# Sample attention with half, sample and head on the partitions, and sample values by column tiles of the PE array

## The reference, cut to what matters

```python
# sample group: DEC_SEQ = 1, 128 samples, 4 heads of 128, 256 memory tokens
qh = q.reshape(bn, t, XA_HEADS, XA_HEAD_DIM)
s = jnp.einsum('bthd,bmhd->bhtm', qh, mem_k)
p = jax.nn.softmax(s * (1.0 / math.sqrt(XA_HEAD_DIM)), axis=-1)
o = jnp.einsum('bhtm,bmhd->bthd', p, mem_v).reshape(bn, t, XA_WIDTH)
z_c = (o * jax.nn.silu(qg)) @ xa_wo
y = (g_a * z_a + g_b * z_b + g_c * z_c) @ w_out
```

## Time and profile before

| | us |
|---|---|
| runs before (median of 3) | 780.32 (775.95 to 801.77) |
| profiled execution, its own time | 778.57 |
| span of its slowest core (core 4) | 777.0 |
| spans of the eight cores | 770.2 to 777.0 |
| granted TensorE clock, core 4 | 0.985 of full |
| busy: PE / PE weight loads / DVE / ACT / POOL | 727.6 / 459.4 / 398.3 / 344.8 / 246.0 |

### The profile page before, as it was taken

One profiled execution on the slowest core, in us unless ns is written; L12 is line 12 of the kernel. 1 busy time (PEld: TensorE's weight loads), 2 busy tenths in 40 slices (PEclk: granted clock), 3 DMA queues, 4 the chain that ended last, 5 costly groups with the idle time before them and its releaser, 6 DMA issues.

```text
span 777.0 us, 13244 instructions; the slowest of 8 cores (770.2 to 777.0 us)
## 1 busy us (share of the span) xinstructions
PE 727.6 (94%) x4884; PEld 459.4 (59%) x4884; DVE 398.3 (51%) x379; ACT 344.8 (44%) x408; POOL 246.0 (32%) x303
## 2 busy tenths in 40 slices
PE   2887999989999989989999999999999999999995
PEld 1555656556566546646666656666666666665442
DVE  3444253747849529727975865546321221223675
ACT  4346378687694776777661211121211112112332
POOL 5555101202103002102023344435464554523211
PEclk9999999999999989989999999999999999999998
DMA  9998934422613322412333694655895848226833
GB/s 201 187 191 148 135 72 40 41 24 19 54 17 35 34 26 28 41 11 29 38 38 72 96 182 80 101 112 65 112 111 68 109 55 74 26 109 217 288 149 139
DMA packets 112618, 69.47 MB, mean 89 GB/s; under 512 B 93987, under 2 KB 100213, under 8 KB 112539
## 3 DMA queue, kind: packets, MB, share of 16 engines
q0 software_dynamic: 99808, 31.60, 40.3%
q1 hardware_dynamic: 12747, 37.03, 14.4%
HBM read 90.53 MB, written 9.82 MB: 129 GB/s over the span
## 4 chain that ended last, share of the span: by engine, by line
PE 84%; DMA 6%; ACT 3%; DVE 2%; issue 2%; POOL 1%; POOLq 0%; SPq 0%; ACTq 0%; DVEq 0%
PE PP L644 72%; PE PP L1211 8%; DMA R<-xp 3%; DMA R<-w_in 3%; PE PP L989 2%; ACT R L847 1%; PE PP L981 1%; DVE R L834 1%; PE PP L1075 1%; ACT R L984 1%; PE PP L1114 0%; POOL R L692 0%; POOL R L702 0%; ACT R L698 0%; PE PP L770 0%
## 5 line engine op out<-in xcount | busy, mean ns | idle before, releaser
L644 PE MATMUL PP<-R 128*128 128x344 bf16 x4104 | 619.7, 311 | 7.7 <-ACT R L847 4.0
L644 PEld LDWEIGHTS PP<-R 128*128 128x128 bf16 x4104 | 399.4, 98 | 216.1 <-issue 19.4
L1163 ACT ACTIVATE R<-PP 128x688 f32<-128x688 f32 x72 | 53.5, 743 | 221.1 <-PE PP L644 188.3
L134 POOL DMA_DIRECT2D R<-w_in x68 | 61.5, 905 | 276.6 <-PE PP L644 265.3
L1172 DVE SCALAR_TENSOR_TENSOR R<-R,PP 128x688 f32<-128x688 f32 x72 | 62.6, 871 | 151.1 <-PE PP L644 137.0
L1211 PE MATMUL PP<-R 128*128 128x512 bf16 (+1 forms) x272 | 59.0, 379 | 0.0
L1176 POOL TENSOR_TENSOR R<-R 128x688 f32<-128x688 f32 x24 | 39.4, 1641 | 36.8 <-DVE R L1172 35.9
L1211 PEld LDWEIGHTS PP<-R 128*128 128x128 bf16 (+1 forms) x272 | 26.4, 97 | 32.3 <-issue 0.4
L834 DVE SCALAR_TENSOR_TENSOR R<-R 128x2048 f32<-128x2048 f32 x18 | 42.3, 2349 | 5.4 <-ACT R L831 4.4
L1181 POOL TENSOR_TENSOR R<-R 128x688 bf16<-128x688 f32 x24 | 39.0, 1641 | 18.4 <-DVE R L1172 18.0
L1220 ACT ACTIVATE R<-R 128x1024 f32<-128x1024 f32 (+1 forms) x17 | 18.0, 1057 | 46.3 <-DVE R L1215 46.3
(11 more groups left out here) (131 smaller groups left out, 592.5 us busy)
## 6 DMA issues: line engine op xcount, KB each, us to landing
R<-w_in POOLq DMA_DIRECT2D x68, 256.0 KB, 5.9
R<-xp SPq DMA_DIRECT2D x32, 512.0 KB, 6.1
R<-ck SPq DMA_DIRECT2D x16, 512.0 KB, 4.4
y_p<-R SPq DMA_DIRECT2D x16, 512.0 KB, 2.9
R<-cv POOLq DMA_DIRECT2D x16, 256.0 KB, 7.4
R<-w_out POOLq DMA_DIRECT2D x8, 256.0 KB, 7.9
R<-xa_wo POOLq DMA_DIRECT2D x14, 128.0 KB, 4.9
R<-lru_wo POOLq DMA_DIRECT2D x8, 192.0 KB, 4.0
```

Of the source, the lines that this page charges most:

```text
L134: eng.dma_start(out=out, in_=in_).then_inc(sems[semkey], 16)
L644: return lambda e: e.matmul(ps.ap[:, b * 512:b * 512 + BLK], lhs(k), rhs[:, k, c:c + BLK], start=(k == 0), stop=(k == nk - 1))
L1163: G.act(lambda e, ps=pg[u], th_=th_: e.activation(out=b3(th_.ap), in_=pv(ps), func=AF.Tanh, scale=0.5), UW, [pg[u].tok], [th_.tok], Px - E ...
```

## The change

Scores: keys come from the host in another layout, so that one load holds 16 tokens of every sample, with token half, sample and head on the 128 partitions (2 x 16 x 4) and 8 tokens x 128 dimensions in each row of 4 KB. The queries are put in that order by two copies and one transpose after the fourth head (`tq`, `qs`, 128 x 128). The multiply reads `qs` from SBUF and repeats it over 8 tokens; the spreading matmuls and the first pair of transposes are gone. The second half's scores are moved from partitions 64 to 127 to 0 to 63 by one DMA within SBUF (`sall`).

Values: each load is again one sample, in rows of 4 KB. `Pm` is widened to 32 columns for each sample, zero but for the 4 columns of its heads. For each four samples 32-column weights from `Pm` stand in four column groups (partitions 32g to 32g + 31 of the PSUM tile), and the values are the moving side, 512 columns: 8 matmuls for four samples, 32 in all. Four results are added up in `Os`, transposed by four 32-bit transposes and gated by four small VectorE operations. There are 7 value buffers in place of 8. Some small tiles move: `qs` now shares space with `pretmp` (L780) and `Ps`, `Pm` with `Sall` and `Es`.

```diff
@@ -432,8 +432,8 @@
     xp = din("xp", [T, D])
     xs = din("xs", [TS, D])
     memp = din("memp", [NM, D])
-    ck = din("ck", [TS, NM, XW])
-    cv = din("cv", [TS, NM, XW])
+    ck = din("ck", [TS, 128, 1024])
+    cv = din("cv", [TS, 128, 1024])
     st_h = din("st_h", [TS, W])
     st_lc = din("st_lc", [TS, 3 * W])
     st_sc = din("st_sc", [TS, 2 * W])
@@ -552,20 +552,21 @@
         m_cinp = front("cinp", 2 + TT, F32)
         SIDE = cur["p"]
         NJS = 6
-        PERM = RB - (XW * 2 + 512 + 256 + 2048 + NJS * TS * 8)
+        PERM = RB - (3072 + NJS * TS * 8)
         assert SIDE + 24672 <= PERM, (SIDE, PERM)
 
         def side(name, off, n, dt):
             return Mem(name, SIDE + off, n, dt)
 
         m_a2 = side("a2", 0, TT, F32)
-        m_qs = Mem("qs", PERM, XW, BF16)
-        m_Sall = Mem("Sall", PERM + 1024, 128, F32)
-        m_Pm = Mem("Pm", PERM + 1536, 128, BF16)
-        m_Es = Mem("Es", PERM + 1792, 256, F32)
-        m_Ps = Mem("Ps", PERM + 2816, 256, F32)
-        m_thS = Mem("thS", PERM + 3840, NJS * TS, F32)
-        m_acS = Mem("acS", PERM + 3840 + NJS * TS * 4, NJS * TS, F32)
+        m_tq = Mem("tq", PERM + 1024, 128, BF16)
+        m_qs = Mem("qs", PERM + 2048, 128, BF16)
+        m_Sall = Mem("Sall", PERM, 256, F32)
+        m_Es = Mem("Es", PERM + 1024, 256, F32)
+        m_Ps = Mem("Ps", PERM + 2048, 256, F32)
+        m_Pm = Mem("Pm", PERM, 1024, BF16)
+        m_thS = Mem("thS", PERM + 3072, NJS * TS, F32)
+        m_acS = Mem("acS", PERM + 3072 + NJS * TS * 4, NJS * TS, F32)
 
         S = Sched(nc)
         G = Graph()
@@ -602,7 +603,7 @@
 
 
         m_prg = Mem("prg", PERM + 1792, 128, F32)
-        m_prt = Mem("prt", PERM + 2816, 128, F32)
+        m_prt = Mem("prt", PERM + 2304, 128, F32)
         prg, prt = m_prg.ap[0:16, :], m_prt.ap[0:66, :]
         t_pg = m_pT.tok("pTg")
         dsem("prg")
@@ -957,12 +958,16 @@
             for u, ps in enumerate(proj(C_Q + hd * 128, P)):
                 G.act(lambda e, ps=ps, u=u: e.copy(out=cols(og[:, hd], u), in_=pv(ps)), UW, [ps.tok], ogt(hd, u * UW, (u + 1) * UW),
                       P - EV + u, psum=True)
+            if hd < 3:
+                return
             P += 8
+            tq = m_tq.ap.rearrange("p (c b h) -> p c b h", c=2, h=4)
+            for c in range(2):
+                G.dve(lambda e, c=c: e.tensor_copy(tq[:, c].rearrange("p b h -> p h b"), og[:, :, T:TT]), 64,
+                      [t_og[i][4] for i in range(4)], [m_tq.t], P)
             ps = Handle(PS)
-            G.pe([lambda e: e.transpose(ps.ap.bitcast(BF16)[0:TS, 0:128], og[:, hd, T:TT], identb)], 0.1,
-                 [t_og[hd][4], m_identb.t], [ps.tok], P)
-            G.dve(lambda e: e.tensor_copy(qs[0:TS, hd * 128:(hd + 1) * 128], ps.ap.bitcast(BF16)[0:TS, 0:128]), 128,
-                  [ps.tok], [m_qs.t], P)
+            G.pe([lambda e: e.transpose(ps.ap.bitcast(BF16)[:, 0:128], m_tq.ap, identb)], 0.1, [m_tq.t, m_identb.t], [ps.tok], P)
+            G.dve(lambda e: e.tensor_copy(qs, ps.ap.bitcast(BF16)[:, 0:128]), 128, [ps.tok], [m_qs.t], P)
 
         def attend(hd, P):
             sg_ = Handle(sgring)
@@ -1061,65 +1066,76 @@
         m_Kb = [Mem(f"Kb{i}", m_wo.off + i * 4096, 1024, F32) for i in range(2)]
         m_prod = Mem("prod", m_wo.off + 8192, 1024, F32)
         m_Va = [Mem(f"Va{i}", m_wo.off + 12288 + i * 2048, 1024, BF16) for i in range(2)]
-        m_Vb = [Mem(f"Vb{i}", m_wo.off + i * 2048, 1024, BF16) for i in range(6)]
+        m_Vb = [Mem(f"Vb{i}", m_wo.off + i * 2048, 1024, BF16) for i in range(5)]
+        m_Os = Mem("Os", m_wo.off + 10240, 512, F32)
 
 
         def sample_scores(P, dP):
             kring, prring = ring("Kb", m_Kb, True), ring("prod", [m_prod])
-            Sall = m_Sall.ap.rearrange("p (c b h) -> p c b h", c=2, b=TS)
-            for b in range(TS):
-                k_, pr_, ps = Handle(kring), Handle(prring), Handle(PS)
-                P1 = P + b * dP
-                G.dma("sp", [(lambda k_=k_: k_.ap.rearrange("p (c f) -> p c f", c=2), ck[b].rearrange("(c m) f -> m c f", c=2))], 524288,
-                      [], [k_.tok], P1 - EV, None)
-                G.pe([lambda e, b=b, ps=ps: e.matmul(ps.ap[:, 0:512], identb[0:TS, b:b + 1].to_broadcast([TS, 128]), qs[0:TS, :],
-                                                     start=True, stop=True)], 0.25, [m_identb.t, m_qs.t], [ps.tok], P1)
-                G.dve(lambda e, k_=k_, pr_=pr_, ps=ps: e.tensor_tensor(
-                    out=pr_.ap.rearrange("p (c f) -> p c f", c=2), in0=k_.ap.rearrange("p (c f) -> p c f", c=2),
-                    in1=ps.ap[:, 0:512].unsqueeze(1).to_broadcast([128, 2, 512]), op=ALU.mult), 1024,
-                    [k_.tok, ps.tok], [pr_.tok], P1)
-                G.dve(lambda e, b=b, pr_=pr_: e.tensor_reduce(out=Sall[:, :, b, :], in_=pr_.ap.rearrange("p (c h d) -> p c h d", c=2, h=4),
+            Sall, sm = m_Sall.ap, m_sm.ap
+            for s in range(TS):
+                k_, pr_ = Handle(kring), Handle(prring)
+                P1 = P + s * dP
+                G.dma("sp", [(lambda k_=k_: k_.ap, ck[s])], 524288, [], [k_.tok], P1 - EV, None)
+                G.dve(lambda e, k_=k_, pr_=pr_: e.tensor_tensor(
+                    out=pr_.ap.rearrange("p (m d) -> p m d", m=8), in0=k_.ap.rearrange("p (m d) -> p m d", m=8),
+                    in1=qs.unsqueeze(1).to_broadcast([128, 8, 128]), op=ALU.mult), 1024, [k_.tok, m_qs.t], [pr_.tok], P1)
+                G.dve(lambda e, s=s, pr_=pr_: e.tensor_reduce(out=Sall[:, s * 8:(s + 1) * 8], in_=pr_.ap.rearrange("p (m d) -> p m d", m=8),
                                                               axis=AX.X, op=ALU.add), 1024, [pr_.tok], [m_Sall.t], P1)
             P2 = P + TS * dP
-            ps = Handle(PS)
-            G.pe([lambda e, c=c: e.transpose(ps.ap[0:64, c * 128:(c + 1) * 128], m_Sall.ap[:, c * 64:(c + 1) * 64], ident)
-                  for c in range(2)], 0.4, [m_Sall.t, m_ident.t], [ps.tok], P2)
-            sm = m_sm.ap
-            G.dve(lambda e: e.tensor_reduce(out=sm[0:64, 0:1], in_=ps.ap[0:64, 0:256], axis=AX.X, op=ALU.max), 256, [ps.tok], [m_sm.t], P2)
+            dsem("sall")
+            G.dma("sp", [(Sall[0:64, 128:256], Sall[64:128, 0:128])], 32768, [m_Sall.t], [m_Sall.t], P2, "sall")
+            Sx = Sall[0:64, :]
+            G.dve(lambda e: e.tensor_reduce(out=sm[0:64, 0:1], in_=Sx, axis=AX.X, op=ALU.max), 256, [m_Sall.t], [m_sm.t], P2)
             G.dve(lambda e: e.tensor_scalar(out=sm[0:64, 0:1], in0=sm[0:64, 0:1], scalar1=-SCALE, scalar2=None, op0=ALU.mult), 1,
                   [m_sm.t], [m_sm.t], P2)
-            G.act(lambda e: e.activation(out=m_Es.ap[0:64, :], in_=ps.ap[0:64, 0:256], func=AF.Exp, scale=SCALE, bias=sm[0:64, 0:1],
-                                         accum_out=sm[0:64, 1:2]), 480, [ps.tok, m_sm.t], [m_Es.t, m_sm.t], P2, EXP, psum=True)
+            G.act(lambda e: e.activation(out=m_Es.ap[0:64, :], in_=Sx, func=AF.Exp, scale=SCALE, bias=sm[0:64, 0:1],
+                                         accum_out=sm[0:64, 1:2]), 480, [m_Sall.t, m_sm.t], [m_Es.t, m_sm.t], P2, EXP)
             G.dve(lambda e: e.reciprocal(out=sm[0:64, 1:2], in_=sm[0:64, 1:2]), 1, [m_sm.t], [m_sm.t], P2)
             G.dve(lambda e: e.tensor_scalar(out=m_Ps.ap[0:64, :], in0=m_Es.ap[0:64, :], scalar1=sm[0:64, 1:2], scalar2=None, op0=ALU.mult),
                   256, [m_Es.t, m_sm.t], [m_Ps.t], P2)
+            Pm = m_Pm.ap.rearrange("p (c b x) -> p c b x", c=2, b=TS)
+            G.dve(lambda e: e.memset(m_Pm.ap, 0.0), 1024, [], [m_Pm.t], P2, mode=2)
             ps2 = Handle(PS)
             G.pe([lambda e, c=c: e.transpose(ps2.ap[:, c * 64:(c + 1) * 64], m_Ps.ap[0:64, c * 128:(c + 1) * 128], ident[0:64, 0:64])
                   for c in range(2)], 0.4, [m_Ps.t, m_ident.t], [ps2.tok], P2)
-            G.dve(lambda e: e.tensor_copy(m_Pm.ap, ps2.ap[:, 0:128]), 128, [ps2.tok], [m_Pm.t], P2)
+            for r in range(4):
+                G.dve(lambda e, r=r: e.tensor_copy(
+                    Pm[:, :, r * 4:r * 4 + 4, r * 4:r * 4 + 4],
+                    ps2.ap[:, 0:128].rearrange("p (c b h) -> p c b h", c=2, h=4)[:, :, r * 4:r * 4 + 4, :]), 32, [ps2.tok], [m_Pm.t], P2)
 
         def sample_values(P, dP):
+
             varing, vbring = ring("Va", m_Va, True), ring("Vb", m_Vb, True)
-            Pm = m_Pm.ap.rearrange("p (c q) -> p c q", c=2)
-            for g in range(4):
+            Pm = m_Pm.ap.rearrange("p (c b x) -> p c b x", c=2, b=TS)
+            Os = m_Os.ap
+            for r in range(4):
                 ps = Handle(PS)
-                for bi in range(4):
-                    b = g * 4 + bi
-                    v_ = Handle(varing if b % 4 == 0 or b == 1 else vbring)
-                    P1 = P + b * dP
-                    G.dma("pool", [(lambda v_=v_: v_.ap.rearrange("p (c f) -> p c f", c=2), cv[b].rearrange("(c m) f -> m c f", c=2))],
-                          524288, [], [v_.tok], P1 - EV, None)
-
```

(40 more changed lines are left out.)

## The result

The changed kernel took 766.41 us (median of 4 runs, 765.93 to 768.38) beside 779.05 for the kernel before on the same chip; the ratio is 0.9856, 95% interval 0.9815 to 0.9896. So by the ratios it is faster by about 10 to 11 us, 1.3 to 1.4%: three times the gain that was forecast (3.3 us on the profiled execution), and just inside the range, which starts at 766. In some executions the four cores of one die run at a lower clock (one run of the kernel before, 801.77 us, is counted among them): the ratios leave these out, and lengths of stages are given from cores 4 to 7 where cores 0 to 3 were disturbed.

A forecast was written before the change was run, and what follows sets the result against it. TensorE, with 84% of the chain, was taken as the bound: 9.8 us leave its list and 5.5 come, 4.3 less; with 1.0 us of added waits, 778.57 - 4.3 + 1.0 = 775.3, predicted 775, range 766 to 786.

The forecast's parts named there:

- rival 4: Between 107 and 437 us a newly planned order wins or loses 4 us and more, 767 to 783; chance 0.12.
- the +1.0 of the forecast: Extra TensorE waits while the scores run in the merge with VectorE full: 1.0 us more than now.
- Value matmuls: On TensorE in the merge: 32 matmuls at 4.3 us, between 1.7 and 6.9, plus 0.8 for switching to narrow weights.
- Dense VectorE stretch: Scores in the merge: VectorE full, 3.1 us a sample, ending about 490; TensorE loses 1.0 us more, lower bound -0.8.
- Softmax wait: TensorE's wait at the second transposes, after the softmax, left at 1.45 us; bounds: gone, or longer by 3.7 us.
- Early part: Three of four query transposes and a copy go: under 1 us, in a part waiting for loads, counted as nothing.
- Rival 1: In the value matmuls the column groups don't overlap, so TensorE's list shortens by only 1.7 us: 778; chance 0.15.
- Rival 2: During the scores VectorE and GpSimd hold each other up and drains come late: 9.6 us together, 785; chance 0.20.
- Rival 3: Value loads come late with seven buffers, 8.5 us for three groups: 784; chance 0.08.

## Why the prediction held, and where its terms were off

The direction and the place held: TensorE's list in the merge got shorter, and the rest follows it. The size was three times the forecast, because four terms were off, all to the same side. By their own bounds each was allowed for. That the range held, by 0.4 us, is partly luck: its lower end took 4 us from another order in the middle part, which gave nothing (rival 4), and left out that with all waits gone the +1.0 of the forecast goes too.

1. **Value matmuls, 4.3 + 0.8 us forecast, 2.2 measured.** With no row of two column groups in flight I took the middle of the bounds. They overlap nearly in full: eight cost 0.55 with the switching, and the switching itself 0.10 rather than 0.20. The estimate from the figure of the Trainium skill, 2.9 for the matmuls, was nearer than the middle. This is the largest miss, 2.9 us. Rival 1 fell with the run in one column group.
2. **Dense VectorE stretch, +1.0 forecast, -0.84 measured.** TensorE lost nothing in it. The bound that I had set aside, the present loss gone, was the outcome. The scores didn't run at 3.1 us a sample either, but at (498.8 - 435.9) / 15 = 4.2, and ended at 501 in place of 490: VectorE was not full, 56.88 of 68 us between 437 and 505; of its idle time 8.0 us ended with a drain's matmul and 1.3 with the landing of keys.
3. **Softmax wait, 1.45 kept, 0 measured.** I saw that L1094 took 2.43 us where its size suggests 0.41, and did not ask why. Had I looked beside it, the GpSimd add would have shown that the wait was an accident of two starts and not a property of the chain.
4. **Early part, 0 forecast, -0.8 to -1.0 measured.** Three query transposes (four before, one now) stood in TensorE's list between the input and the keys, and were not hidden by loads.

-3.3 us forecast and 2.9 + 1.8 + 1.45 + 0.9 = 7.1 of misses make -10.4; the merge and the early part measure -9.1 - 0.9 = -10.0, the ratios -11.2 and -10.0.

**Rival 2, VectorE and GpSimd.** The mechanism is there, the cost is not. Lines L1080 (the multiply) and L1192 (a GpSimd add) of the changed kernel, ns min/median/max and first and last start:

```profile
L1080 DVE TENSOR_TENSOR R<-R x16: 1207/1225/2296, 435.9 to 498.8; 128x1024 f32<-128x1024 f32 x16
...
L1192 POOL TENSOR_TENSOR R<-R x24: 1632/1640/2613, 439.5 to 685.9; 128x688 f32<-128x688 f32 x24
```

and their meetings in the timeline, with the normalisation:

```profile
461.27 2.30 DVE L1080 TENSOR_TENSOR R<-R 128x1024 f32<-128x1024 f32 x1
...
459.25 3.23 POOL L1197 TENSOR_TENSOR R<-R 128x688 bf16<-128x688 f32 x2
...
481.77 5.83 POOL L1197 TENSOR_TENSOR R<-R 128x688 bf16<-128x688 f32 x3 [0.87 <-DVE R L1188]
...
483.87 2.23 DVE L1080 TENSOR_TENSOR R<-R 128x1024 f32<-128x1024 f32 x1
...
510.36 0.69 DVE L1095 TENSOR_SCALAR R<-R 64x256 f32<-64x256 f32 x1 [0.18 <-DVE R L1094]
...
509.26 1.64 POOL L1192 TENSOR_TENSOR R<-R 128x688 f32<-128x688 f32 x1 [0.78 <-DVE R L1090]
```

The multiply at 461.27 stands until the add ends at 462.48 and then takes its 1.1 us; at 483.87 each holds the other. Over all 16 multiplies that is 23.0 us in place of 19.5: 3.5 us of VectorE where I had counted 5.3, in a stretch with 11 us to spare. The drains L1188 keep their 0.87 us mean (58.9 us for 68), and TensorE waits for none on this core. The Trainium skill, "SBUF — State Buffer", section "Who interferes with whom", has both cases: a VectorE instruction with two SBUF inputs contends with a GpSimd one that reads SBUF, and so can a `tensor_scalar`, in a mode that takes two ports, with one blocked while the other holds the ports. The multiply of 2.30 us agrees with the first, the normalisation that ends 0.15 us after the add with the second. I had used the first half of that section and not the second, which bore on a wait that stood in the earlier trace rows.

Late drains can cost time all the same. On core 0 of the run with the other order within a group, three loads of keys landed 9.5, 8.4 and 5.7 us after their issue, the scores held up the drains behind them on VectorE, and between 470 and 510 us, ahead of the values, TensorE waited 2.3 us for two drains. The merge of that core took 266.1 us. One row of its chain, and its waits:

```profile
477.51 8.41 DMA R<-ck
...
PE PP L645 <- DVE R L1188: 2.3, 2, 1.6
```

**Rival 3** fell: TensorE is busy 38.00 of 38 us while the values run, with loads of 7.5 us. **Rival 4** fell: the stretch from the prompt's keys to the last product of branch B has a median of 334.6 us in both kernels.
